# Sixty-four chunk turns ahead of the first FFN: a matmul against a scaled diagonal replaced by a scaling on GpSimd and a transpose on TensorE

## The chip, the cores and the metric

The kernel runs on one core of one Trainium2 chip. The metric is the device time of one execution in microseconds, median of several runs. The kernel before takes 2605.58 us (three runs, 2605.37 to 2605.85).

## The reference

Four sub-layers run one after another over a stream `x` of 1024 tokens by 1024 channels, float32: an HGRN2 mixer, a SwiGLU FFN, a short-convolution mixer, a second FFN. Between the mixer's output and the FFN stands the part that matters here:

```
x  = x + g1 * _rmsnorm(y, norm_w[l, 1])                     # y: output projection of the mixer
hf = _modulate(_rmsnorm(x, norm_w[l, 2]), sh2, sc2)         # h * (1 + scale) + shift, per channel
x  = x + g2 * _rmsnorm(_swiglu(hf, ffn_w_in[l], ffn_w_out[l]), norm_w[l, 3])

def _rmsnorm(x, w):
    xf = x.astype(jnp.float32)
    y = xf * lax.rsqrt(jnp.mean(xf * xf, axis=-1, keepdims=True) + EPS)
    return (y * w.astype(jnp.float32)).astype(x.dtype)
```

The division by a token's root mean square is one number per token; scale and shift are one number per channel. There are 256 context tokens too, in the first mixer alone.

## The kernel before

The stream is held as eight blocks (`LAT` = 8) of 128 tokens by 1024 channels, tokens in the partitions. The FFN wants channels in the partitions, so every block is turned in eight chunks of 128 by 128. Turns are counted by instance: 0 is the input of the first mixer, 1 the first FFN's, 2 the convolution's, 3 the second FFN's. All products are float32 split into a high and a low part, three matmuls for each product (hi times hi, lo times hi, hi times lo). The FFN's products are a Strassen scheme of seven kinds, M1 to M7; each needs its own combination of the input's quarters (`x_terms`), split into high and low.

The norm's factor reaches the block in one of two ways. Where the instance is in `SCALED` (2 and 3), ScalarE writes the block times `x_rstd` into a buffer (`scaled_of`), and TensorE transposes the chunks of that (L1435, `pe.transpose` against `ident`). Instances 0 and 1 leave the block as it is: VectorE writes a diagonal matrix of the 128 factors (L2750, `diag`), and TensorE multiplies every chunk by that (L1436), which scales and turns in one. In the trace such a float32 matmul of one chunk is two records.

Instance 1 runs inside the first output projection. No scheduler decides the order: each engine has its own written list, and semaphores tie them. For block tb of 0 to 7:

- TensorE (`projection_blocks`): wait for `proj_evac` of block tb-2 and for its factor (`diag_done`), `turn_block` of block tb-2 in two halves of four chunks (banks 4 and 5), then what is left of the projection of block tb, `proj_full`. Blocks 6 and 7 are turned at the end: 6 ahead of the first FFN product, 7 inside the third product (`turns_at`).
- ScalarE (`projection`): `y_norm` (square and sum of the projection, square root, `y_std`), `turned_raw` of block tb-1 (eight copies from PSUM with scale and shift into `raw_b`), `x_norm` (the same on the new stream block, `x_std`), then `x_highs` of block tb-1: two for blocks 0 to 3, four for blocks 4 to 7.
- VectorE (`projection`): reciprocal `y_rstd`, `proj_scaled`, the new block `xt`, then `x_sums` of block tb-1 (one, or three from block 4 on), `x_norm` (reciprocal `x_rstd`, and `diag`), `x_lows` of block tb-1 (two, or four).
- GpSimd (`ffn_units`): for the FFN's kind M6, `x6(block)` for blocks 4 to 7, three instructions each (sum, cast to the high part, low part), each as soon as its block's `raw_b` stands. Then the sums and low parts of the weight units.

The FFN's first 14 products run in `FIRST_ORDER`: M2 and M4 of units 0 and 1, then M3, M5, M1, M7, M6. M2 and M4 read blocks 0 to 3 alone; M3, M5, M1, M7 read up to block 7 (`x_ready`), M6 reads what GpSimd made (`x6_ready`). SyncE's queue reloads a slot `xt` for block tb+4 when block tb is turned, and loads the first FFN weights (`ffn_raw`) when all are.

Of the kernel before, what the change touches and what calls it, by code (L numbers as in the profile page):

```python
# [10 lines left out]
ALU = mybir.AluOpType  # L11
# [11 lines left out]
LAT = SEQ // P  # L23
# [64 lines left out]

EARLY_Y, EARLY_SCALE, EARLY_ADD = ({first + 2 * tb: tb for tb in range(4)} for first in (60, 61, 62))
EARLY_X, EARLY_RSTD, EARLY_SCALED = ({first + 2 * tb: tb for tb in range(4)} for first in (63, 64, 65))  # L90
SCALED = 2, 3
CONV_HIGHS = 55, 58
FIRST_TURN = 68

# [92 lines left out]
T0 = (0, 20, 36, 52)  # L187
D0 = (0, 10, 18, 26)
# [3 lines left out]
def turns(inst):  # L192
    return TURNS[(0, 1, 2, 1)[inst]]


def block_turns(inst, block):

    return T0[inst] + 2 * block, T0[inst] + 2 * block + 1
# [92 lines left out]
def normed(inst):  # L291
    return NORMED[0 if inst == 0 else 1]


def blocks_of(q):
    return (8, 9) if q == CTX_Q else (2 * q, 2 * q + 1)


def turned_after(inst, block):

    if inst % 2:
        return block_turns(inst, block)[1] + 1
    return T0[inst] + max(t for t, (q, f) in enumerate(turns(inst)) if block in blocks_of(q)) + 1
# [85 lines left out]
def build_trunk(nc, x, ctx, cond, ada, ada_bias, norm_w, lb_raw, gnorm, conv_w,  # L389
# [8 lines left out]
    def at(name, kib, shape, dt=F32):  # L398
        return nc.alloc_sbuf_tensor_at(name, shape, dt, offset=base + int(kib * 1024))
# [144 lines left out]
    ident = at("ident", 214, [P, P])  # L544
# [4 lines left out]
    def small(name, n):  # L549
        t = at(name, small_at[0], [P, n])  # L550
        small_at[0] += (4 * n + 31) // 32 * 32 / 1024
        return t
# [21 lines left out]
    x_squares, x_std, x_rstd = (small("x_squares", LAT + CCH), small("x_std", LAT + CCH),  # L574
                                small("x_rstd", LAT + CCH))
# [11 lines left out]
    with ctx_mgr:  # L587
# [25 lines left out]
        S = {n: ctx_mgr.enter_context(nc.semaphore(n)) for n in names}  # L613
# [117 lines left out]
        def diag_of(inst, block):  # L731
            i = normed(inst).index(block)
            return diag_start[:, i % 6, :] if inst == 0 else diag[:, i % 4, :]

        def scaled_of(inst, block):

            return ys[0][block // 4][:, block % 4, :] if inst == 2 else x_scaled[block % 3][:, :]

        def stream(inst, block):

            if block >= LAT:
                return ctxt[:, block - LAT, :]
            if inst == 0:
                return x_start[:, block, :]
            return xt_end[0][:, block, :] if inst == 2 else xt_slots[inst // 2][block % 4][:, :]
# [53 lines left out]
        block = ctx_mgr.enter_context(nc.Block())  # L799
# [363 lines left out]
        def _(pool):  # L1163
# [102 lines left out]
            for n in range(4, N_HGRN_OUT):  # L1266
                h, i = n // HEAD_PANELS, n % HEAD_PANELS
# [8 lines left out]
            for half in range(2):  # L1276
# [9 lines left out]
            pool.tensor_tensor(hgrn_rows[KB - 1][1][:, :], last_row_raw[:, :], hgrn_rows[KB - 1][0][:, :], ALU.subtract  # L1286
                               ).then_inc(S["panel_split"], 1)

            def ffn_units(f):

                k0 = PAIR_UNITS * f
# [28 lines left out]

                pool.sem_inc(S["unit_summed"], 2 * len(SUMMED))
                pool.sem_inc(S["unit_ready"], 2 * len(SUMMED))
                if f == 1:
                    pool.wait_ge(S["proj_full"], LAT * (f + 1))
                for block in LATE:
                    x6(block)
# [70 lines left out]
        def _(pe):  # L1397
# [34 lines left out]
            def turn_chunk(out_ap, inst, block, kb):  # L1432

                if inst in SCALED:
                    return pe.transpose(out_ap, chunk(scaled_of(inst, block), kb), ident[:, :])  # L1435
# [634 lines left out]
        def _(act):  # L2070
# [430 lines left out]
            def projection(sub, inst):  # L2501

                f = sub // 2
                if f == 1:
                    out_row_copy(sub)
                act.wait_ge(S["mods_ready"], 2 * inst)
                for tb in range(LAT):
                    act.wait_ge(S["proj_full"], LAT * f + tb + 1)
                    y_norm(sub, tb, proj_of(f, tb), junk_proj[f])
                    if tb > 0:  # L2510
                        turned_raw(inst, tb - 1)
                    act.wait_ge(S["x_updated"], LAT * sub + tb + 1)
                    x_norm(inst, tb, junk_proj[f])
                    if tb > 0:
                        x_highs(f, tb - 1, IN_TIME[f])
                    if inst in SCALED:
                        scale_x(inst, tb)

            def ffn(f):
# [183 lines left out]
        def _(dve):  # L2703
            V = nc.vector
# [28 lines left out]
            def x_norm(inst, block):  # L2733

                n = D0[inst] + normed(inst).index(block)
                c = slice(block, block + 1)
                dve.wait_ge(S["x_std_done"], n + 1)
                V.reciprocal(x_rstd[:, c], x_std[:, c]).then_inc(S["x_rstd_done"], 1)
                if inst in SCALED:
                    return  # L2740
                dve.wait_ge(S["x_rstd_done"], n + 1)
                i = normed(inst).index(block)
                ring_of = 6 if inst == 0 else 4
                if i >= ring_of:
                    dve.wait_ge(S["turned"], turned_after(inst, normed(inst)[i - ring_of]))
                elif inst > 0:
                    dve.wait_ge(S["turned"], T0[inst])
                if inst == 0 and i < 4:
                    return
                V.tensor_scalar(diag_of(inst, block), ident[:, :], x_rstd[:, c], None, ALU.mult  # L2750
                                ).then_inc(S["diag_done"], 1)

            def low(inst, t):
                dve.wait_ge(S["h_hi_done"], H0[inst] + t + 1)
# [61 lines left out]
            for tb in range(4):  # L2816
                x_norm(0, tb)
# [623 lines left out]
```

## Time and profile before

| | |
|---|---|
| device time, median of three | 2605.58 us |
| span of the profiled execution | 2600.0 us |
| TensorE busy (matmuls) | 2524.9 us, 97% |
| VectorE, ScalarE, GpSimd busy | 1750.5, 1122.8, 1245.5 us |
| first output projection and turn of its blocks | about 864 to 935 us of the span |
| FFN products without a pause from | 935.37 us |

The profiled execution's span is 2600.0 us; 5.6 us of the median lie around it. "Busy" of an engine is the time with an instruction in flight; matmuls overlap, so a row's duration (0.39 us) is longer than the step from one to the next (0.23 us). The chain of waits follows the work that ended last back to the start. A timeline lists instructions in order of time, with the idle time ahead of each and what ended it. Line numbers are those of the kernel before; L2707 (VectorE) and L2072 (ScalarE) are helpers, so their rows are told apart by the tile they write.

### The profile page before, as it was taken

The page shows a single profiled execution, that of the slowest core. Times are in us where ns is not written, and L with a number is a line of the kernel's source. Part 1 is how long each engine was busy: PE and PEld are TensorE (multiplying, and loading weights), DVE is VectorE, ACT ScalarE, POOL GpSimd, SP SyncE. Part 2 cuts the span into 40 slices and gives each one's busy share as a digit, 9 for nine tenths or more (in the row PEclk, how much of TensorE's full clock was granted, in tenths as well). Part 3 has the DMA queues.
Part 4 walks back from the last instruction along what each step waited for, and adds up shares of the span by engine and source line. Part 5 has one row for each costly group of instructions (what it writes and reads, how often), then busy time and mean ns, then how long its engine had stood idle before and what let it go on. Part 6 is the DMA issues. An engine that isn't in the chain of part 4 may idle for free.

```text
span 2600.0 us, 35820 instructions
## 1 busy us (share of the span) xinstructions
PE 2524.9 (97%) x12452; PEld 2115.7 (81%) x12452; DVE 1750.5 (67%) x2343; ACT 1122.8 (43%) x2124; POOL 1245.5 (48%) x811
## 2 busy tenths in 40 slices
PE   7999999999999989999999999999999999999998
PEld 5888888888878778888888877888787888888886
DVE  5377777767865566667667986666436555565888
ACT  5334534443443653343445475111264333434444
POOL 3121321432230037776768952444304776766983
PEclk8999999999999999999999999999999999999999
DMA  6223431441361343343456332333514323345533
GB/s 261 74 74 121 178 136 67 154 146 65 114 264 61 138 141 130 122 145 129 165 204 238 97 110 97 115 112 113 214 54 154 106 89 109 116 166 216 191 99 114
DMA packets 119634, 351.05 MB, mean 135 GB/s; under 512 B 12240, under 2 KB 12240, under 8 KB 116432
## 3 DMA queue, kind: packets, MB, share of 16 engines
q1 hardware_dynamic: 119504, 349.33, 38.1%
q8 instruction: 80, 1.31, 0.2%
q14 instruction: 50, 0.41, 0.0%
HBM read 258.58 MB, written 90.70 MB: 134 GB/s over the span
## 4 chain that ended last, share of the span: by engine, by line
PE 83%; DVE 7%; POOL 3%; ACT 3%; DMA 2%; issue 1%; SPq 1%; DVEq 0%; ACTq 0%; POOLq 0%
PE psum L1402 19%; PE psum L1403 19%; PE psum L1404 19%; PE psum L1975 4%; PE psum L1977 4%; PE psum L1976 4%; PE psum L1650 2%; PE psum L1652 2%; PE psum L1651 2%; PE psum L1602 2%; POOL row_unit_sum L1358 2%; PE psum L1616 1%; PE psum L1589 1%; PE psum L1572 1%; DVE k_all L2999 1%
## 5 line engine op out<-in xcount | busy, mean ns | idle before, releaser
L1402 PE MATMUL psum<-x_hi,unit 128*128 128x512 f32 x1232 | 481.5, 391 | 5.2 <-DVE x_lo L2707 5.2
L1403 PE MATMUL psum<-x_lo,unit 128*128 128x512 f32 x1232 | 480.0, 390 | 0.0
L1404 PE MATMUL psum<-x_hi,unit 128*128 128x512 f32 x1232 | 479.9, 390 | 0.0
L2707 DVE TENSOR_TENSOR c_set<-c_set,psum 128x512 f32<-128x512 f32 x352 | 233.8, 685 | 279.3 <-ACT c_set L2072 178.6
L1308 POOL TENSOR_TENSOR unit<-unit_sum,unit 128x512 fp32r<-128x512 f32 x200 | 294.4, 1480 | 5.8 <-ACT unit L2072 4.9
L1402 PEld LDWEIGHTS psum<-x_hi,unit 128*128 128x128 f32 x1232 | 231.9, 188 | 54.2 <-ACT c_set L2072 5.7
L1404 PEld LDWEIGHTS psum<-x_hi,unit 128*128 128x128 f32 x1232 | 231.7, 188 | 48.5
L1403 PEld LDWEIGHTS psum<-x_lo,unit 128*128 128x128 f32 x1232 | 231.9, 188 | 47.6
L1402 PE MATMUL psum<-h_hi,w_hi 128*128 128x512 f32 x624 | 262.6, 421 | 0.2 <-DVE h_lo L2707 0.2
L1975 PE MATMUL psum<-row_unit_hi,part_hi 128*128 128x512 f32 x616 | 241.8, 392 | 3.1 <-DVE part_lo L2707 1.8
L1404 PE MATMUL psum<-h_hi,w_lo 128*128 128x512 f32 x624 | 244.1, 391 | 0.0
L1403 PE MATMUL psum<-h_lo,w_hi 128*128 128x512 f32 x624 | 243.9, 391 | 0.0
L1977 PE MATMUL psum<-row_unit_hi,part_lo 128*128 128x512 f32 x616 | 240.5, 390 | 0.0
L1976 PE MATMUL psum<-row_unit_lo,part_hi 128*128 128x512 f32 x616 | 240.3, 390 | 0.0
L2707 DVE TENSOR_TENSOR part_lo<-part_raw,part_hi 128x512 fp32r<-128x512 f32 x154 | 186.1, 1211 | 64.0 <-ACT part_hi L2072 63.5
L2072 ACT ACTIVATE c_set<-psum 128x512 f32<-128x512 f32 x176 | 100.3, 597 | 265.3 <-PE psum L1404 265.3
L1302 POOL TENSOR_TENSOR unit_sum<-ffn_raw 128x512 f32<-128x512 f32 x80 | 108.6, 1357 | 197.2 <-PE psum L1402 197.2
L1302 POOL TENSOR_TENSOR unit_sum<-ffn_raw,ffn_raw 128x512 f32<-128x512 f32 x120 | 159.8, 1332 | 58.5 <-PE psum L1402 58.0
L1222 POOL TENSOR_TENSOR w_lo<-w_raw,w_hi 128x1024 fp32r<-128x1024 f32 x30 | 73.5, 2449 | 238.6 <-ACT w_hi L2072 238.6
L2072 ACT ACTIVATE unit<-unit_sum 128x512 fp32r<-128x512 f32 x200 | 126.0, 630 | 55.8 <-POOL unit_sum L1302 55.8
L1975 PEld LDWEIGHTS psum<-row_unit_hi,part_hi 128*128 128x128 f32 x616 | 116.1, 188 | 29.4 <-issue 3.4
L1402 PE MATMUL psum<-conv_h_hi,conv_w_hi 128*128 128x512 f32 x352 | 138.1, 392 | 0.4 <-POOL conv_w_lo L1207 0.4
(320 smaller groups left out, 5630.9 us busy)
## 6 DMA issues: line engine op xcount, KB each, us to landing
ffn_raw<-in_w_ffn_in SPq DMA_DIRECT2D x80, 512.0 KB, 5.1
part_raw<-parts_kept SPq DMA_DIRECT2D x154, 256.0 KB, 2.7
parts_kept<-part_sums SPq DMA_DIRECT2D x22, 1280.0 KB, 5.3
out_raw<-in_w_ffn_out SPq DMA_DIRECT2D x44, 512.0 KB, 7.4
w_raw<-in_w_hgrn_in SPq DMA_DIRECT2D x40, 512.0 KB, 3.6
ada_raw<-in_ada SPq DMA_DIRECT2D x32, 512.0 KB, 4.8
conv_ada_raw<-in_ada SPq DMA_DIRECT2D x32, 512.0 KB, 4.1
units_kept<-stage_unit SPq DMA_DIRECT2D x28, 512.0 KB, 2.9
```

The source lines that it names most:

```text
L1222: pool.tensor_tensor(place[1][:, :], w_raws[0][:, slot, :], place[0][:, :], ALU.subtract).then_inc(S["panel_split"], 1)
L1302: pool.tensor_tensor(units[(PRODUCTS * e + l) % 4][2][:, :], one, other, op).then_inc(S["unit_summed"], 1)
L1308: pool.tensor_tensor(unit[1][:, :], unit[2][:, :], unit[0][:, :], ALU.subtract).then_inc(S["unit_ready"], 1)
L1358: pool.tensor_tensor(row_unit(n)[2][:, :], one, other, op).then_inc(S["rows_summed"], 1)
L1402: begin = pe.matmul(out_ap, hi[:, a:b], rhs_hi, start=first, stop=False)
L1403: pe.matmul(out_ap, hi[:, a:b], rhs_lo, start=False, stop=False)
L1404: return begin, pe.matmul(out_ap, lo[:, a:b], rhs_hi, start=False, stop=last)
L1975: begin = pe.matmul(dst, of_hi[:, tokens], hi[:, :], start=g == 0, stop=False)
L1976: pe.matmul(dst, of_hi[:, tokens], lo[:, :], start=False, stop=False)
L1977: return begin, pe.matmul(dst, of_lo[:, tokens], hi[:, :], start=False, stop=g == FFN_GROUPS - 1)
L2072: nc.scalar.activation(dst, src, func, **kw).then_inc(S[sem], 1)
L2707: V.tensor_tensor(dst, a, b, op).then_inc(S[sem], 1)
```

## The change

Instance 1 joins `SCALED`, and GpSimd does the scaling. For each of the eight blocks it waits for `x_rstd`, writes block times factor into one of three buffers `x_scaled` (from the fourth block on also waiting until the block three earlier is turned), and only then TensorE transposes the chunks. VectorE no longer writes `diag` for instance 1. GpSimd does the eight scalings ahead of its twelve `x6` instructions, which so come after the last block's scaling.

```diff
-SCALED = 2, 3
+SCALED = 1, 2, 3
...
+            def scale_x(inst, block):
+                pool.wait_ge(S["x_rstd_done"], D0[inst] + normed(inst).index(block) + 1)
+                if block >= 3:
+                    pool.wait_ge(S["turned"], turned_after(inst, block - 3))
+                pool.tensor_scalar(scaled_of(inst, block), stream(inst, block), x_rstd[:, block:block + 1], None, ALU.mult
+                                   ).then_inc(S["diag_done"], 1)
...
-                if f == 1:
+                if f == 0:
+                    for tb in range(LAT):
+                        scale_x(1, tb)
+                else:
                     pool.wait_ge(S["proj_full"], LAT * (f + 1))
                 for block in LATE:
                     x6(block)
...
-                    if inst in SCALED:
+                    if inst == 3:
                         scale_x(inst, tb)
...
-                if inst in SCALED:
-                    return
-                dve.wait_ge(S["x_rstd_done"], n + 1)
...
+                if inst == 0:
+                    dve.wait_ge(S["x_rstd_done"], n + 1)
...
```

GpSimd's list at the projection, before. `x_6` is the input of kind M6, `raw_b` the turned block with scale and shift:

```order
L1286 TENSOR_TENSOR hgrn_row_96<-last_row_raw,hgrn_row_96 128x1024 [waits w_hi_done]
L1315 TENSOR_TENSOR x_6_sum<-raw_b_137 128x4x128 [waits modulated]
L1317 CAST x_6_hi<-x_6_sum 128x4x128 [waits x6_summed]
L1319 TENSOR_TENSOR x_6_lo<-x_6_sum,x_6_hi 128x4x128 [waits x6_hi]
L1315 TENSOR_TENSOR x_6_sum<-raw_b_137 128x4x128 [waits modulated]
L1317 CAST x_6_hi<-x_6_sum 128x4x128 [waits x6_summed]
```

The same place now:

```order
L1286 TENSOR_TENSOR hgrn_row_96<-last_row_raw,hgrn_row_96 128x1024 [waits w_hi_done]
L1294 TENSOR_SCALAR x_scaled_128<-xt_0_145,x_rstd 128x1024 [waits x_rstd_done]
L1294 TENSOR_SCALAR x_scaled_129<-xt_1_146,x_rstd 128x1024 [waits x_rstd_done]
L1294 TENSOR_SCALAR x_scaled_130<-xt_2_147,x_rstd 128x1024 [waits x_rstd_done]
L1294 TENSOR_SCALAR x_scaled_128<-xt_3_148,x_rstd 128x1024 [waits turned,x_rstd_done]
L1294 TENSOR_SCALAR x_scaled_129<-xt_0_145,x_rstd 128x1024 [waits turned,x_rstd_done]
L1294 TENSOR_SCALAR x_scaled_130<-xt_1_146,x_rstd 128x1024 [waits turned,x_rstd_done]
L1294 TENSOR_SCALAR x_scaled_128<-xt_2_147,x_rstd 128x1024 [waits turned,x_rstd_done]
L1294 TENSOR_SCALAR x_scaled_129<-xt_3_148,x_rstd 128x1024 [waits turned,x_rstd_done]
L1323 TENSOR_TENSOR x_6_sum<-raw_b_137 128x4x128 [waits modulated]
L1325 CAST x_6_hi<-x_6_sum 128x4x128 [waits x6_summed]
```

The eight scalings stand in front, and all twelve `x_6` instructions come behind the eighth.

VectorE's list for one block of the projection, before (`x_0` and `x_1` are the inputs of kinds M2 and M4):

```order
L2707 TENSOR_TENSOR x_1_sum<-raw_b_137 128x4x128 [waits modulated]
L2738 RECIPROCAL x_rstd<-x_std 128x1 [waits x_std_done]
L2750 TENSOR_SCALAR diag<-ident,x_rstd 128x128 [waits turned,x_rstd_done]
L2707 TENSOR_TENSOR x_0_lo<-raw_b_137,x_0_hi 128x4x128 [waits x_hi]
L2707 TENSOR_TENSOR x_1_lo<-x_1_sum,x_1_hi 128x4x128 [waits x_hi]
L2777 RECIPROCAL y_rstd<-y_std 128x1 [waits y_std_done,x_loaded0]
```

and now:

```order
L2718 TENSOR_TENSOR x_1_sum<-raw_b_137 128x4x128 [waits modulated]
L2749 RECIPROCAL x_rstd<-x_std 128x1 [waits x_std_done]
L2718 TENSOR_TENSOR x_0_lo<-raw_b_137,x_0_hi 128x4x128 [waits x_hi]
L2718 TENSOR_TENSOR x_1_lo<-x_1_sum,x_1_hi 128x4x128 [waits x_hi]
L2784 RECIPROCAL y_rstd<-y_std 128x1 [waits y_std_done,x_loaded0]
```

Only `diag` is gone. On TensorE every list position stays, and `L1436 psum<-diag,xt` becomes a transpose `psum<-ident,x_scaled` at the same place with the same waits.

## Rows read from the trace of the kernel before

**Rows 1.** The page: the span.
```profile
span 2600.0 us, 35820 instructions
```
**Rows 2.** Busy time by stretch: bounds, length, each engine, TensorE's granted clock, DMA.
```profile
870.00:920.00 50.00, 39.18 (x192) 30.08 (x191) 41.52 (x60) 45.16 (x108) 8.16 (x6) 0.91 0.42 146
```
**Rows 3.** Chain of waits, one block's round: start, duration, engine, tile.
```profile
885.20 0.30 ACT y_std L2072
885.79 1.30 DVE proj_scaled L2788
...
891.92 0.30 ACT y_std L2072
```
**Rows 4.** VectorE's timeline, block 2's factor: start, duration, instruction, idle before.
```profile
883.16 0.16 DVE L2738 RECIPROCAL x_rstd<-x_std 128x1 f32<-128x1 f32 x1 [0.86 <-ACT x_std L2072]
883.36 0.29 DVE L2750 TENSOR_SCALAR diag<-ident,x_rstd 128x128 f32<-128x128 f32 x1
...
884.29 0.69 DVE L2707 TENSOR_TENSOR x_lo<-x_sum,x_hi 128x512 fp32r<-128x512 f32 x1
885.59 0.17 DVE L2777 RECIPROCAL y_rstd<-y_std 128x1 f32<-128x1 f32 x1 [0.62 <-ACT y_std L2072]
```
**Rows 5.** VectorE's timeline, blocks 4 to 7.
```profile
901.77 3.38 DVE L2707 TENSOR_TENSOR x_sum<-raw_b 128x512 f32<-128x512 f32 x3
...
905.08 0.15 DVE L2738 RECIPROCAL x_rstd<-x_std 128x1 f32<-128x1 f32 x1
905.26 1.10 DVE L2750 TENSOR_SCALAR diag<-ident,x_rstd 128x128 f32<-128x128 f32 x1
...
906.88 1.88 DVE L2707 TENSOR_TENSOR x_lo<-x_sum,x_hi 128x512 fp32r<-128x512 f32 x3
908.69 0.15 DVE L2777 RECIPROCAL y_rstd<-y_std 128x1 f32<-128x1 f32 x1
...
911.33 4.44 DVE L2707 TENSOR_TENSOR x_sum<-raw_b 128x512 f32<-128x512 f32 x3
915.70 0.15 DVE L2738 RECIPROCAL x_rstd<-x_std 128x1 f32<-128x1 f32 x1
...
918.50 0.15 DVE L2777 RECIPROCAL y_rstd<-y_std 128x1 f32<-128x1 f32 x1
...
921.59 3.41 DVE L2707 TENSOR_TENSOR x_sum<-raw_b 128x512 f32<-128x512 f32 x3 [0.36 <-ACT raw_b L2072]
924.92 0.15 DVE L2738 RECIPROCAL x_rstd<-x_std 128x1 f32<-128x1 f32 x1
```
**Rows 6.** GpSimd's timeline at the projection.
```profile
911.24 1.30 POOL L1315 TENSOR_TENSOR x_sum<-raw_b 128x512 f32<-128x512 f32 x1 [4.96 <-ACT raw_b L2072]
...
930.69 1.30 POOL L1315 TENSOR_TENSOR x_sum<-raw_b 128x512 f32<-128x512 f32 x1 [4.54 <-ACT raw_b L2072]
...
955.06 1.29 POOL L1302 TENSOR_TENSOR unit_sum<-ffn_raw 128x512 f32<-128x512 f32 x1 [20.38 <-PE psum L1402]
```
**Rows 7.** TensorE's timeline: turns of blocks 2, 6, 7 (half), and M3's start.
```profile
883.74 2.02 PE L1436 MATMUL psum<-diag,xt 128*128 128x128 f32 x16 [0.18 <-issue]
...
916.23 3.78 PE L1436 MATMUL psum<-diag,xt 128*128 128x128 f32 x16 [4.73 <-DVE diag L2750]
...
926.43 1.06 PE L1436 MATMUL psum<-diag,xt 128*128 128x128 f32 x8
...
935.37 0.47 PE L1402 MATMUL psum<-x_hi,unit 128*128 128x512 f32 x1 [2.19 <-DVE x_lo L2707]
```
**Rows 8.** GpSimd's groups over the whole span: busy us, mean ns of one.
```profile
L1204 POOL TENSOR_TENSOR conv_w_hi<-conv_w_raw,zero 128x1024 fp32r<-128x1024 f32 x22 | 48.4, 2200 | 162.5 <-DMA conv_w_raw<-in_w_conv_in 98.2 <-PE psum L1402 63.7 <-DVE part_lo L2707 0.6
...
L1168 POOL MEMSET cond_pad<- 128x1024 f32 x1 | 1.0, 952 | 0.0
```
**Rows 9.** GpSimd's timeline, a cast that runs alone.
```profile
1950.17 0.61 POOL L1317 CAST x_hi<-x_sum 128x512 fp32r<-128x512 f32 x1
```
**Rows 10.** Chain of waits: four transposes of 128 by 128.
```profile
853.79 0.44 PE psum L1639 x4
```

More of the change, by code:

```diff
@@ L2738, in x_norm @@
                 V.reciprocal(x_rstd[:, c], x_std[:, c]).then_inc(S["x_rstd_done"], 1)
-                if inst in SCALED:
-                    return
-                dve.wait_ge(S["x_rstd_done"], n + 1)
[L2742 to L2751, printed above, removed]
+                if inst == 0:
+                    dve.wait_ge(S["x_rstd_done"], n + 1)
+                    i = normed(inst).index(block)
+                    if i >= 6:
+                        dve.wait_ge(S["turned"], turned_after(inst, normed(inst)[i - 6]))
+                    if i < 4:
+                        return
+                    V.tensor_scalar(diag_of(inst, block), ident[:, :], x_rstd[:, c], None, ALU.mult
+                                    ).then_inc(S["diag_done"], 1)
             def low(inst, t):
```

## The prediction

> **What bounds the kernel now.** I read the page first: TensorE is busy nearly all of the span [rows 1], so a change counts only where TensorE pauses or where work leaves it. Then the busy time by stretch: in 870 to 920 us TensorE is busy for 39.18 of 50 us while ScalarE has 45.16 and VectorE 41.52 [rows 2]; from 935.37 on the FFN's products run without a pause [rows 7]. So the gain or loss of this change is one number: how far the start of M3, at 935.37, moves. Everything behind it is TensorE's own list and moves with it.
>
> Third, the chain of waits inside that stretch. From block 2 on it does not run through TensorE. It is a round between ScalarE and VectorE: `y_std`, then VectorE's `proj_scaled` and `xt`, then ScalarE's `x_norm`, and the next `y_std` 6.72 us later (885.20 to 891.92) [rows 3]. The turns lie beside it: ScalarE picks up block 2's turned chunks just behind `y_std`, at 885.5, and TensorE had begun that turn at 883.74 [rows 7]. From block 4 on the round is longer and VectorE carries it: its three `x_sums` take 3.38, 4.44 and 3.41 us, where three instructions of the same shape take 1.88 when nothing disturbs them [rows 5]. What disturbs them is GpSimd's `x6`, begun at 911.24 beside the sums of 911.33 [rows 6]; a `diag` takes 1.10 us beside it instead of 0.29 [rows 4, 5]. The two engines take turns on whole instructions.
>
> The Trainium skill says the same under SBUF — State Buffer, Who interferes with whom: a VectorE instruction with two SBUF inputs and a GpSimd instruction that reads SBUF block each other for a whole instruction. It speaks against this change too, since the scaling is such an instruction and `x_lows` follow at once; no more comes of it here than the sum below holds already.
>
> **The change, part by part.**
>
> *The transposes.* Four cost 0.44 us [rows 10], so a block 0.88; a block's turn before is sixteen records in 2.02 us at full clock (about 1.8 without the tail that overlaps the next instruction), and 3.78 us for block 6, behind a pause of 4.73 us [rows 7]. TensorE is not what the round waits for, so of some 8 us of TensorE time next to nothing is gained directly; half a turn of block 7 is on the path: 0.44 against 0.9 (half of 1.8), **-0.45**.
>
> *The scaling's price s.* The trace has no such GpSimd instruction. Lower end: a MEMSET of the same width, 0.95 us [rows 8]. A cast of half the width alone takes 0.61 [rows 9]; twice that is 1.22 with its fixed part counted twice. Upper end: a 1024-wide instruction with two operands, one of them a broadcast column, 2.20 us [rows 8]. The scaling has one wide input and one output, as the cast has, so I take **s = 1.1**, and keep 0.95 to 2.2.
>
> The Trainium skill, GPSIMD Engine Reference, Elementwise — side-by-side cycle accounting, gives 1.03 cycles an element for a body of up to two operations and about 1.8 for a tight loop. At 1.2 GHz these are estimates of 0.9 and 1.5 us. The undisturbed cast is nearer the first; by the second the sum would be near zero, which is the second rival.
>
> *Early rounds, the factors of blocks 1 to 4 (four links).* Before, block 2's reciprocal ends at 883.32, the two `x_lows` end at 884.98, and VectorE then idles 0.62 us for `y_std`, starting `y_rstd` at 885.59 [rows 4]. Now GpSimd starts at 883.4 and holds off the `x_lows` until 884.5; these take 0.60 and 0.69 and end at 885.8, so `y_rstd` is late by 0.2. The first half of the turn is there at 884.5 + 0.44 = 884.95, still ahead of ScalarE at 885.5. Four times 0.2: **+0.8**. Block 0's scaling (about 1.1 instead of 0.3) ends within the shorter turn it pays with: 0.
>
> *The three groups of sums.* GpSimd no longer runs `x6` beside them, since all of it stands behind the eighth scaling. (3.38 - 1.88) + (4.44 - 1.88) + (3.41 - 1.88) = **-5.6** [rows 5].
>
> *Late rounds.* From the reciprocal of `x_rstd` to `y_rstd` VectorE now does reciprocal, one `x_low` or the scaling's hold, then the rest: 0.2 + 1.1 + 4 times 0.61 = 3.75. Before it was 905.08 to 908.69 = 3.6 (with a `diag` of 1.10), and 915.70 to 918.50 = 2.8 [rows 5]. **+0.1 and +0.95**. Last, block 7: from the reciprocal at 924.92 to its turn at 926.43 were 1.5 us, of which TensorE's products filled part [rows 5, 7]; now 0.2, up to 0.6 until a running `x_low` lets go, and 1.1: **+0.4**. TensorE comes to this turn earlier too, as block 6's turn is ready about 3 us sooner.
>
> *`x6` behind the scalings.* Four blocks of `x6`, some 4 us each, now run from about 922.5 to 938.5, beside block 6's lows and block 7's add, sum and lows. Before only the last of them did (from 930.69 [rows 6]). The path 926.43 to 935.37 already holds disturbed instructions; more of them can hold it by one or two GpSimd instructions: 0 to 1.5, I take **+0.5**. M6 itself is TensorE's ninth product; with M3 at 932 and four products of 12 times 0.23 us between, it is wanted at 943. GpSimd then has nothing to do until 955 less the gain, where it idled 20.38 us [rows 6]. So the later `x6` costs nothing else.
>
> *The rest.* ScalarE's list is the same. SyncE issues no other DMA; its loads of `xt` slots and of `ffn_raw` wait for turns, which move by less than 1 us for blocks 0 to 3 and come earlier for the last. Removing `diag` from VectorE: 0.29 in the early rounds lay in idle time, the 1.10 is counted in the link.
>
> **Sum:** -0.45 + 0.8 - 5.6 + 0.1 + 0.95 + 0.4 + 0.5 = **-3.3 us**. M3 starts at 932.1, the span is 2596.7; with the 5.6 us that the median has around the profiled span (2605.6 against 2600.0) the time is **2602.3 us**.
>
> With s at 0.95 and nothing for `x6` the sum is about -4.9; s counts in seven links (four early, two late, block 7), so s = 2.2 gives -3.3 + 7 times 1.1 = +4.4.
>
> **The rivals.**
>
> *A, the slower one: GpSimd's scaling becomes the link.* If GpSimd takes the column of factors as a second operand, s is 2.2, or 2.4 with disturbance. For it: the broadcast rows of 2.20 do just that. Against it: the cast. The first half of the turn is then at 883.4 + 2.2 + 0.44 = 886.0, behind ScalarE's 885.5, and the `x_lows` end at 886.9, 1.3 late, each round. The break-even is 1.1 + 3.3/7 = 1.6 us for one scaling; at 2.2 to 2.4 the time is 2610.0 to 2611.5. Chance 0.18.
>
> *B, nothing to be seen:* s of 1.5 to 1.9. -3.3 + 7 times 0.4 to 0.8 = -0.5 to +2.3, 2605 to 2608. Chance 0.20. Here also belongs the case that the gain at M3 is given back later, for which I see no place.
>
> *C, more than forecast:* s near 1.0, `x6` disturbs nothing, and the pauses that put TensorE on the low clock (block 6's 3.78) go away. -4.9 and the 0.36 us wait of VectorE at 921.59 [rows 5], with the shorter pauses: -5 to -6, 2600. Chance 0.14.
>
> *D, `x6` late for M6:* GpSimd would have to end at 943 or later, 4.5 us behind the estimate; each further us comes back. -2 to +1. Chance 0.05.
>
> TensorE, before, came out of each of the pauses ahead of blocks 5 and 6 at a low clock (the stretch's mean grant is 0.91 [rows 2]). The Trainium skill, TensorE: Matmul & The Clock Gate, PE-mode transpose, says that transposes do not count as busy to the clock gate, which would leave the first products at 1.2 GHz a little longer. The products ahead of block 7's turn have to wait for its scaling in any case, so it would change neither sum nor chance.
>
> **How the numbers follow.** The forecast (s up to 1.4, -4.9 to -1.2) has 0.43. A measurement of this kernel can tell about 0.2%, 5.2 us, from no change. Faster by more: most of C, and a little of the forecast whose terms all err to one side, 0.15. Slower by more needs s over 2.3, or A with more disturbance: 0.15. Within: 0.70. The range 2599.9 to 2610.0 leaves out the better half of C and the worse half of A.
>
> **What would show it.** Right: GpSimd rows `x_scaled` near 1.1 us; the three `x_sums` near 1.9 us each group; reciprocals `x_rstd` of blocks 5, 6, 7 at about 904.5, 913, 921.5 instead of 905.08, 915.70, 924.92; M3 near 932. Wrong: scaling rows of 1.6 us and more with rounds longer than 7 us in blocks 1 to 4; sums still over 3 us; TensorE waiting for `x_6_lo` at M6; or M3 early and the second half of the kernel longer.

## The result: eleven microseconds slower

The changed kernel takes 2616.51 us (median of 4 runs, 2614.58 to 2616.71) against 2605.47 us of the kernel before on the same chip (4 runs, 2604.93 to 2605.85): ratio 1.0044, 95% interval 1.0032 to 1.0056. The forecast was 2602.3 us, its range ended at 2610.0. Both the number and the sign were wrong.

The page of the changed kernel, its span, to set beside [rows 1]:

```profile
span 2615.0 us, 35689 instructions
```

Busy time by stretch, changed kernel (bounds, length, TensorE, its weight loads, VectorE, ScalarE, GpSimd, granted clock, DMA), beside [rows 2]:

```profile
870.00:920.00 50.00, 33.72 (x136) 22.88 (x135) 33.52 (x44) 37.87 (x92) 17.98 (x6) 0.93 0.46 158
```

Every engine but GpSimd has less to show for the same 50 us: ScalarE 37.87 instead of 45.16, VectorE 33.52 instead of 41.52. Fewer rounds fit into the stretch. What fills the time stands in GpSimd's timeline (start, duration, instruction, idle time before and what ended it):

```profile
881.24 2.85 POOL L1294 TENSOR_SCALAR x_scaled<-xt,x_rstd 128x1024 f32<-128x1024 f32 x1 [5.33 <-DVE x_rstd L2749]
889.41 2.85 POOL L1294 TENSOR_SCALAR x_scaled<-xt,x_rstd 128x1024 f32<-128x1024 f32 x1 [5.33 <-DVE x_rstd L2749]
...
914.38 3.75 POOL L1294 TENSOR_SCALAR x_scaled<-xt,x_rstd 128x1024 f32<-128x1024 f32 x1 [5.77 <-DVE x_rstd L2749]
```

One scaling takes **2.85 us**, where the forecast had 1.1 and at most 2.2. The first five take that, the last three 3.75, with a group of three of VectorE's lows beside them. The scalings follow each other at 8.17 us (881.24 to 889.41), where a round was 6.72 before [rows 3]. The chain of waits of the stretch names who carries it:

```profile
877.84 1.75 ACT raw_b L2083 x5
879.58 1.05 ACT junk_proj L2083 x2
...
880.65 0.30 ACT x_std L2083
...
880.98 0.17 DVE x_rstd L2749
...
881.24 2.85 POOL x_scaled L1294
```

Before, the chain went from ScalarE's `y_std` to VectorE's `proj_scaled` and back, with the turns beside it [rows 3]. Its round of 6.72 us is as long as ScalarE's own list of one block; in ScalarE's timeline of the kernel before no row of that round has idle time ahead of it:

```profile
885.40 2.89 ACT L2072 ACTIVATE raw_b<-psum,mods,in_scale 128x128 f32<-128x128 f32 x8
888.37 1.06 ACT L2072 ACTIVATE junk_proj<-xt 128x1024 f32<-128x1024 f32 x1
...
892.13 2.89 ACT L2072 ACTIVATE raw_b<-psum,mods,in_scale 128x128 f32<-128x128 f32 x8
```

Now the chain goes reciprocal, scaling, turn, `raw_b`, `x_norm`, and the next block's reciprocal. ScalarE's timeline shows the turn as what it waits for, and TensorE's shows the turn right behind the scaling:

```profile
883.02 0.29 ACT L2083 ACTIVATE y_std<-y_squares,eps 128x1 f32<-128x1 f32 x1
884.85 2.91 ACT L2083 ACTIVATE raw_b<-psum,mods,in_scale 128x128 f32<-128x128 f32 x8 [1.54 <-PE psum L1446]
...
888.83 0.29 ACT L2083 ACTIVATE x_std<-x_squares,eps 128x1 f32<-128x1 f32 x1
```

```profile
884.19 1.06 PE L1446 MATMUL psum<-ident,x_scaled 128*128 128x128 f32 x8 [2.60 <-issue]
...
937.65 0.66 PE L1446 MATMUL psum<-ident,x_scaled 128*128 128x128 f32 x4
...
946.87 0.77 PE L1413 MATMUL psum<-x_hi,unit 128*128 128x512 f32 x1 [3.32 <-DVE x_lo L2718]
```

**The ring.** Scaling from 881.24 to 884.09, first half of the turn, `raw_b` from 884.85, `x_norm` behind it, `x_std` at 888.83, reciprocal at 889.15, next scaling at 889.41. All of it but the scaling is 8.17 - 2.85 = 5.32 us. So the ring is s + 5.32 (s is the price of one scaling, as in the prediction), and it replaces the round of 6.72 as soon as s is above 1.4. The forecast gave each early round only what `x_lows` and `y_rstd` lose to a running GpSimd instruction.

What was meant to be gained did come. VectorE's timeline, against the 4.44 and 3.41 of [rows 5]:

```profile
912.32 1.90 DVE L2718 TENSOR_TENSOR x_sum<-raw_b 128x512 f32<-128x512 f32 x3 [1.64 <-ACT raw_b L2083]
914.13 0.16 DVE L2749 RECIPROCAL x_rstd<-x_std 128x1 f32<-128x1 f32 x1
914.81 2.73 DVE L2718 TENSOR_TENSOR x_lo<-x_sum,x_hi 128x512 fp32r<-128x512 f32 x3
...
933.60 0.15 DVE L2749 RECIPROCAL x_rstd<-x_std 128x1 f32<-128x1 f32 x1
```

**A better mark than M3.** The forecast measured everything by the start of M3, since "everything behind it is TensorE's own list and moves with it". GpSimd's first `unit_sum` waits for a product behind M3. It started at 955.06 before [rows 6], 19.69 us behind M3, and now at 968.41, 21.54 us behind:

```profile
968.41 1.29 POOL L1310 TENSOR_TENSOR unit_sum<-ffn_raw 128x512 f32<-128x512 f32 x1 [15.11 <-PE psum L1413]
```

The stretches behind M3 of the changed kernel say why: TensorE was busy all the time, but the clock granted to it was low at first (a mean of 0.63 of full speed over 4.5 us).

```profile
946.87:951.37 4.50, 4.50 (x13) 3.62 (x14) 4.50 (x5) 1.26 (x2) 4.35 (x4) 0.63 0.38 117
951.37:955.87 4.50, 4.50 (x22) 3.72 (x21) 2.67 (x4) 2.51 (x3) 1.85 (x2) 1.00 0.72 243
```

and the same 4.5 us of the kernel before:

```profile
935.37:939.87 4.50, 4.50 (x20) 3.75 (x21) 3.55 (x6) 2.71 (x4) 0.00 (x0) 1.00 0.46 140
```

Thirteen matmuls instead of twenty, seven of 0.23 us: some 1.6 us are lost behind M3's start. So below the stage is measured from the first `y_rstd` of the projection (865.89 before, 868.51 now) to the first `unit_sum`: 89.17 us before, 99.90 after, **+10.7**, close to the 11.0 between the times. Measured from its own trace's `y_rstd`, the stage leaves out what varies ahead of it: that reciprocal starts anywhere between 865.7 and 869.0 us in the fourteen traces of this study, although the kernels don't differ ahead of it. What lies behind `unit_sum` varies too, by 2.4 us (1644.7 to 1647.1).

### The profile page after: what moved, and what is told of

Read it like the earlier page. It is cut to its first block, busy times and chain, and to the rows that moved or that the text cites. A ratio compares the mean times of both kernels' runs of the same rounds, so it can differ in the third digit from the quotient of the medians.

```text
span 2615.0 us, 35689 instructions
## 1 busy us (share of the span) xinstructions
PE 2527.5 (97%) x12388; PEld 2113.1 (81%) x12388; DVE 1750.0 (67%) x2335; ACT 1121.8 (43%) x2124; POOL 1269.5 (49%) x819
## 4 chain that ended last, share of the span: by engine, by line
PE 82%; DVE 6%; POOL 4%; issue 3%; ACT 3%; DMA 2%; SPq 1%; DVEq 0%; ACTq 0%; POOLq 0%
PE psum L1413 19%; PE psum L1415 19%; PE psum L1414 19%; PE psum L1986 4%; PE psum L1988 4%; PE psum L1987 4%; PE psum L1661 2%; PE psum L1663 2%; PE psum L1662 2%; PE psum L1613 2%; POOL row_unit_sum L1369 2%; PE psum L1600 1%; PE psum L1627 1%; PE psum L1583 1%; DVE k_all L3006 1%
## 5 line engine op out<-in xcount | busy, mean ns | idle before, releaser
L1222 POOL TENSOR_TENSOR w_lo<-w_raw,w_hi 128x1024 fp32r<-128x1024 f32 x30 | 73.1, 2437 | 238.4 <-ACT w_hi L2083 238.4
```

The source lines that it names most:

```text
L1222: pool.tensor_tensor(place[1][:, :], w_raws[0][:, slot, :], place[0][:, :], ALU.subtract).then_inc(S["panel_split"], 1)
```

## The experiments

Theory 1: the loss comes from the price of the scaling instruction, through the ring. Rivals: moving `x6` costs it, or GpSimd standing in the ring costs it at any price, or the transposes do. All differences of time are against the kernel before on the same chip. The stage is cut into four parts, each as change against before, in us: **early** from `y_rstd` to block 4's reciprocal `x_rstd` (30.72 before), **late** from there to block 7's (28.31), **last** from there to M3 (10.45), **clock** from M3 to `unit_sum` (19.69).

| kernel | one scaling | round | early | late | last | clock | stage | time |
|---|---|---|---|---|---|---|---|---|
| changed | 2.85 GpSimd | 8.17 | +6.27 | -0.21 | +2.82 | +1.85 | +10.73 | +11.0 |
| changed_again | 2.85 | 8.17 | +6.64 | -0.17 | +2.83 | +1.84 | +11.14 | +11.3 |
| x6_between | 2.84 | 8.16 | +6.41 | +0.50 | +1.96 | +1.95 | +10.82 | +9.6 |
| two_operand | 1.89 | 7.48 | +3.22 | -2.93 | +1.18 | +1.91 | +3.38 | +2.4 |
| half_scales | 1.57 | 6.90 | +1.16 | -3.61 | +1.92 | +1.94 | +1.41 | +1.2 |
| copy_scales | 1.04 | 6.72 | +0.07 | -5.35 | +0.31 | +1.90 | -3.07 | -2.4 |
| act_scales | 1.13 ScalarE | 7.76 | +3.91 | -2.69 | +1.31 | +1.42 | +3.95 | +5.9 |
| dve_scales | 0.75 VectorE | 6.72 | -0.24 | -5.78 | +1.61 | +1.65 | -2.76 | -2.3 |
| no_scaling | none | 6.72 | -0.58 | -5.82 | +0.75 | +2.45 | -3.20 | -3.4 |
| x6_late | diag as before | 6.72 | -0.01 | -5.81 | +2.65 | +3.06 | -0.11 | -2.5 |
| late_fill | diag as before | 6.72 | 0.00 | -5.81 | +2.55 | +0.10 | -3.16 | -2.4 |
| dve_fill | 0.75 VectorE | 6.72 | -0.24 | -5.76 | +1.52 | +0.05 | -4.43 | -3.4 |

The stage comes from one trace, the time from medians whose runs lie 4 to 7 us apart; they agree within about 2.5 us throughout. Differences of time up to some 3.5 us reach the edge of their intervals or lie within them, so comparisons as fine as that rest on the stage. The kernel with ten more GpSimd instructions (prices, below) was run once and serves for its rows alone. The rows below are those on which a verdict rests.

**The price by itself.** The kernel before, with ten GpSimd instructions of five forms behind block 0's reciprocal.

```diff
+forms = (lambda: pool.tensor_scalar(dst[:, :], src[:, :], col, None, ALU.mult),
+         lambda: pool.tensor_scalar(dst[:, :], src[:, :], 2.0, None, ALU.mult),
+         lambda: pool.tensor_scalar(dst[:, 0:HALF], src[:, 0:HALF], col, None, ALU.mult),
+         lambda: pool.tensor_copy(dst[:, :], src[:, :]),
+         lambda: pool.tensor_tensor(dst[:, :], src[:, :], col.broadcast_to([P, D]), ALU.mult))
```

> The kernel before with ten GpSimd instructions put into its idle time ahead of the first x6, each waiting for the one before, on a buffer of ones: twice tensor_scalar 1024 wide with a column of factors, the same with a constant, 512 wide with the column, tensor_copy 1024, tensor_tensor against the broadcast column. If the price of 2.85 us is the column's, the constant is near the copy (about 1.1); if it is tensor_scalar's own, the constant takes 2.85 too; 512 columns give 1.5 either way; the tensor_tensor 1.9.

GpSimd's timeline, the first of two rows for each form:

```profile
873.34 2.85 POOL L1331 TENSOR_SCALAR x_scaled<-x_scaled,x_rstd 128x1024 f32<-128x1024 f32 x1
876.27 2.77 POOL L1332 TENSOR_SCALAR x_scaled<-x_scaled 128x1024 f32<-128x1024 f32 x1
879.14 1.60 POOL L1333 TENSOR_SCALAR x_scaled<-x_scaled,x_rstd 128x512 f32<-128x512 f32 x1
880.80 1.10 POOL L1334 COPY x_scaled<-x_scaled 128x1024 f32<-128x1024 f32 x1
881.99 1.90 POOL L1335 TENSOR_TENSOR x_scaled<-x_scaled,x_rstd 128x1024 f32<-128x1024 f32 x1
```

The price belongs to the operation: 2.77 with a constant, 2.85 with the column. A copy, which moves the same bytes, takes 1.10, and the form with two operands 1.90. The second row of each form, in the same order, is 4.22, 2.77, 1.98, 1.04 and 2.35 us: VectorE was at work beside all ten instructions, and beside the longest of them, from 883.98 on, it ran a sum, a `diag` and two lows. 2.85 is thus the lower of two values, and the one that the first five scalings of the changed kernel show. The forecast had taken the cast as the nearest row, with "one wide input and one output, as the cast has". For GpSimd the count of inputs does not order these forms. The Trainium skill, GPSIMD Engine Reference, Elementwise — side-by-side cycle accounting, gives 1.03 cycles an element for a body of up to two operations and 2.6 for two inputs; at 1.2 GHz these are estimates of 0.9 and 2.2 us. The copy is near the first. The scaling, one operation on one wide input, stands at three times it, and there the measurement decides against the page. The two-operand form stands below the second, but its second operand is a broadcast column. With two full inputs of this width the kernel before has `w_lo<-w_raw,w_hi` (GpSimd, L1222, 30 rows), 2.38 us and more, which agrees with the second.

**The scaling in other forms, at its place.**

```diff
-pool.tensor_scalar(scaled_of(inst, block), stream(inst, block), x_rstd[:, block:block + 1], None, ALU.mult
-                   ).then_inc(S["diag_done"], 1)
+pool.tensor_tensor(scaled_of(inst, block), stream(inst, block),              # two_operand
+                   x_rstd[:, block:block + 1].broadcast_to([P, D]), ALU.mult).then_inc(S["diag_done"], 1)
+pool.tensor_copy(scaled_of(inst, block), stream(inst, block)).then_inc(S["diag_done"], 1)   # copy_scales
```

> The changed kernel with the scaling written as a tensor_tensor against the broadcast column of factors, which took 2.2 us in other places of this kernel, instead of 2.85. Theory 1 (the scaling's duration s counts in some seven links): 7 times 0.65 = 4.5 us under the changed kernel, about 2612. Theory 2 (not the scaling): no difference, 2616.5.

> The changed kernel with GpSimd's eight scalings replaced by plain copies of the block into the same buffers, at the same places and with the same waits. It leaves out the norm's factor on the first FFN's input. A copy of this size took 1.10 us undisturbed in the run of single prices, which is the price the prediction assumed for a scaling. Theory 1 (only the price of the instruction makes the change slow): the ring is 1.10 + 5.32 = 6.42 us, under the round of 6.72 us, so blocks 1 to 4 keep 6.72 us, the groups of three sums stay at 1.9 us, the reciprocals of blocks 5, 6 and 7 end near 904.5, 912.5 and 921, M3 starts near 931 to 932.5, and the time is 3 +- 1.5 us below the kernel before, as forecast for s = 1.1. Theory 2 (that GpSimd stands in the ring at all costs, whatever its price, by taking turns with VectorE): rounds over 7 us, M3 behind 935, time at or above the kernel before.

> The changed kernel with GpSimd scaling only the first four chunks of a block (512 columns, 1.60 us undisturbed in the run of single prices); the last four chunks are transposed from the block itself, so half of the channels lack the norm's factor. The ring is 1.60 + 5.32 = 6.92 us, just above 6.72. Theory 1: rounds of blocks 1 to 4 of 6.9 to 7.2 us, so 1 to 2 us are lost there and the gain of the sums just about pays for it: M3 at 933 to 936, time within 2 us of the kernel before, between copy_scales and two_operand (1.90 us, rounds 7.48, M3 939.6). Theory 2 (no threshold, each microsecond counts from zero): four rounds longer than those of copy_scales by the whole 0.5 us each.

Times: two_operand 2606.5 us against 2604.06, ratio 1.0013 (1.0004 to 1.0022); half_scales 2605.85 against 2604.68, 1.0006 (0.9997 to 1.0015); copy_scales 2602.33 against 2604.68, 0.9991 (0.9982 to 1.0). GpSimd's timeline in half_scales:

```profile
884.45 1.56 POOL L1294 TENSOR_SCALAR x_scaled<-xt,x_rstd 128x512 f32<-128x512 f32 x1 [5.32 <-DVE x_rstd L2749]
891.35 1.57 POOL L1294 TENSOR_SCALAR x_scaled<-xt,x_rstd 128x512 f32<-128x512 f32 x1 [5.33 <-DVE x_rstd L2749]
```

and in copy_scales, with VectorE's last lows there:

```profile
886.54 1.04 POOL L1294 COPY x_scaled<-xt 128x1024 f32<-128x1024 f32 x1 [5.68 <-DVE x_rstd L2748]
893.26 1.04 POOL L1294 COPY x_scaled<-xt 128x1024 f32<-128x1024 f32 x1 [5.68 <-DVE x_rstd L2748]
```

```profile
920.91 1.89 DVE L2717 TENSOR_TENSOR x_sum<-raw_b 128x512 f32<-128x512 f32 x3
922.72 0.15 DVE L2748 RECIPROCAL x_rstd<-x_std 128x1 f32<-128x1 f32 x1
924.44 4.49 DVE L2717 TENSOR_TENSOR x_lo<-x_sum,x_hi 128x512 fp32r<-128x512 f32 x3
```

Rounds of 6.90 at 1.57 (1.57 + 5.33) and of 6.72 at 1.04 (where s + 5.32 would be 6.36) agree with a threshold at 1.4. No price between 1.04 and 1.57 was run. At 1.04 GpSimd idles 5.68 instead of 5.33 us: the older round is back in charge. So theory 1 holds and "GpSimd in the ring at any price" falls. The sizes expected held for copy_scales and half_scales; for two_operand about 2612 us was expected by seven links of 0.65, and it took 2606.5, about twice that gain; its scalings were cheaper by 0.96 us early and by 1.86 in the last three blocks (1.89 for 3.75), not by 0.65. two_operand's rounds of 7.48 are 0.27 above 1.89 + 5.32. VectorE's and ScalarE's timelines show the forecast's other mechanism there:

```profile
888.16 2.16 DVE L2718 TENSOR_TENSOR x_lo<-raw_b,x_hi 128x512 fp32r<-128x512 f32 x1 [0.36 <-ACT x_hi L2083]
...
893.62 1.06 ACT L2083 ACTIVATE junk_proj<-xt 128x1024 f32<-128x1024 f32 x1 [0.17 <-DVE xt L2718]
```

Beside GpSimd's instruction (887.89 to 889.78) an `x_lo` of 0.69 takes 2.16 us, `y_rstd` and `xt` follow it late, and `x_norm`, which read a waiting `xt` in the ring, now waits for it. With copies nearly the forecast's own case was run (1.04 for s = 1.1). Of its four early links, 0.2 each, the last lies behind block 4's reciprocal and so in the late part. Early is +0.07 where +0.6 was forecast, late -5.35 where -4.35 was, last +0.31 where +0.45 was, and then +1.90 behind M3, where nothing was.

**The same kernel once more.**

> The changed kernel once more, unaltered, beside the two others on one chip: 9 to 12 us slower than the kernel before, scalings of 2.85 us, rounds of 8.17 us in blocks 1 to 4, M3 near 946.9. It shows how far the start of M3 and the time move from one profile to another, as a measure for the differences read between the variants.

2615.98 us against 2604.68, ratio 1.0040 (1.0025 to 1.0056). Its stage differs by 0.4 us from the first trace, in one early round of 8.54 us, whose turn took 1.85 us instead of 1.06. That is the measure for the table's differences.

**`x6` alone, and `x6` back in between.**

```diff
                 if f == 1:
                     pool.wait_ge(S["proj_full"], LAT * (f + 1))
+                else:                                              # x6_late, in the kernel before
+                    pool.wait_ge(S["x_rstd_done"], D0[1] + LAT)
...
                     for tb in range(LAT):
                         scale_x(1, tb)
+                        if tb > 4:                                 # x6_between, in the changed kernel
+                            x6(tb - 1)
+                    x6(LAT - 1)
```

> The kernel before with one edit: GpSimd waits for the eighth x_rstd before its first x6 instruction. Diagonals and matmuls stay. Theory 1 (the changed kernel lost by the price of GpSimd's scaling; putting x6 back was a gain as forecast): the three groups of x_sums fall from 3.38, 4.44, 3.41 us to about 1.9 each, M3 starts 5 to 6 us sooner, time 5 to 6.5 us under before. Theory 2 (x6 behind the last block is what cost): M3 or M6 waits, time 3 us or more over before.

> The changed kernel with x6 of block 4 behind the scaling of block 5, of block 5 behind that of block 6, of block 6 behind that of block 7, instead of all behind the eighth. Theory 1 (the price of the scaling, 2.85 us in a ring scaling, turn, raw_b, x_norm, x_rstd): nothing of that ring changes, time within 3 us of the changed kernel's 11 over before. Theory 2 (x6 standing behind the last scaling holds up VectorE ahead of M3): 4 us or more better than the changed kernel.

x6_late: 2601.52 us against 2604.06, ratio 0.9991 (0.9982 to 1.0). x6_between: 2613.66 against 2604.03, 1.0038 (1.0024 to 1.0052). VectorE's timeline of x6_late:

```profile
917.32 1.90 DVE L2709 TENSOR_TENSOR x_sum<-raw_b 128x512 f32<-128x512 f32 x3
...
919.32 1.43 DVE L2752 TENSOR_SCALAR diag<-ident,x_rstd 128x128 f32<-128x128 f32 x1
...
921.27 4.47 DVE L2709 TENSOR_TENSOR x_lo<-x_sum,x_hi 128x512 fp32r<-128x512 f32 x3
```

Moving `x6` alone gives the -5.8 us of the late part, and x6_between, with the price of 2.85 and `x6` early, is as slow as the changed kernel. So the move isn't the loss. (x6_between has -0.86 of the changed kernel's last part and +0.71 in the late one.) But the move fell short of the 5 to 6.5 us expected of it, and took 2.5: it takes part of its gain back twice: the last block's `diag` takes 1.43 and its lows 4.47 us beside `x6` (last +2.65, where the forecast had +0.5 for `x6`), and the rest goes to the clock, below.

**The scaling on other engines, or none.** act_scales lets ScalarE write `x_scaled` as it does for instance 3; dve_scales puts this on VectorE in place of `diag`:

```diff
+V.tensor_scalar(scaled_of(inst, block), stream(inst, block), x_rstd[:, c], None, ALU.mult
+                ).then_inc(S["diag_done"], 1)
```

no_scaling transposes the block itself; its first FFN's input lacks the norm's factor.

> ScalarE writes the scaled block for instance 1 (as it does for instances 2 and 3, 1.14 us each) and GpSimd does x6 after the eighth x_rstd; TensorE transposes. Theory 1: the scaling is cheap as latency but ScalarE is the engine that is full in the rounds of blocks 1 to 4, so these grow by up to 1.1 us each; with the freed sums the time ends 0 to 4 us over before. Theory 3 (only the latency of the scaling counts, not whose list it stands in): 1.1 us is what was forecast for GpSimd, so 2 to 4 us under before.

> VectorE writes the scaled block in place of the diagonal (0.5 us for 512 columns elsewhere, so 0.7 to 0.8 here, against 0.29), x6 after the eighth x_rstd, TensorE transposes. Theory 1: the ring stays under ScalarE's round of 6.72 us; VectorE had 0.6 us to spare in each early round; so like the kernel with only x6 moved, 1 to 3.5 us under before. If transposes in place of diagonals cost by themselves, over before.

> The changed kernel without the scaling: TensorE transposes the unscaled blocks as soon as x_rstd is there, x6 after the eighth x_rstd; the norm's factor is left out of the first FFN's input. It has the shorter turns and the late x6, and no price at all. Theory 1: 5 to 7 us under before, about 2599. Theory 2: still 5 us or more over before.

act_scales: 2609.92 us against 2604.03, ratio 1.0020 (1.0010 to 1.0029). dve_scales: 2601.71 against 2604.03, 0.9986 (0.9977 to 0.9996). no_scaling: 2600.7 against 2604.06, 0.9987 (0.9978 to 0.9997). ScalarE has no idle time in act_scales' early rounds, one of which is 7.76 us:

```profile
888.43 1.14 ACT L2082 ACTIVATE x_scaled<-xt,x_rstd 128x1024 f32<-128x1024 f32 x1
...
896.20 1.13 ACT L2082 ACTIVATE x_scaled<-xt,x_rstd 128x1024 f32<-128x1024 f32 x1
```

That is 6.72 plus the 1.04 from one ScalarE row to the next, so in this kernel ScalarE's list sets the early round. act_scales was expected to end 0 to 4 us over the kernel before and ended 5.9 over; dve_scales came as expected. The transposes cost nothing that these rows show; with the whole change done by VectorE at 0.75 us a block, the early rounds stay at 6.72. And even with no scaling at all, only 3.2 us are to be had in this stage, where 5 to 7 were expected: M3 starts 5.65 us sooner, and 2.45 of it are lost behind.

**The clock behind the last pause.** late_fill is x6_late, and dve_fill dve_scales, with twelve matmuls in TensorE's list ahead of the wait for M3's input. They write the bank that M3's first product overwrites.

```diff
                         if first and kb == 0:
+                            if f == 0 and kind == M3:
+                                for _ in range(12):
+                                    pe.matmul(bank(b), units[slot][0][:, 0:P], xs[f][M2][0][:, 0, :], start=True, stop=True)
                             x_done(kind)
```

> x6_late (the kernel before with only GpSimd's x6 behind the eighth factor) with twelve matmuls of 128x512 more in TensorE's list right ahead of its wait for M3's input, into the bank that M3 overwrites; they use weights and an input that are there. In x6_late M3 started 3.2 us sooner than before (counted from the first y_rstd of its own trace), behind a pause of 2.76 us, and then TensorE ran about 6 us at a granted clock of 0.50, so that GpSimd's first unit_sum, which waits for a product behind M3, came at the same distance as before (89.06 against 89.17 us). Theory 1 (the gain at M3 was given back by the clock that fell after the pause): twelve matmuls at full clock last 2.7 us and fill the pause; M3 starts where it did (66.3 us after y_rstd), at a granted clock of 1.00, unit_sum comes 2.5 to 3 us sooner (86.3), and the time falls by another 2 to 3 us, 4 to 5 below the kernel before. Theory 2 (the late x6 or VectorE's copies hold M3's first products, or the clock falls whatever TensorE does): granted clock of M3 and the distance to unit_sum as in x6_late, same time or a little more.

> The same twelve matmuls in dve_scales (the change's transposes, VectorE doing the scaling, x6 behind the last factor), where M3 started 65.07 us after y_rstd behind a pause of 3.10 us and unit_sum came at 86.41, M3's first 16 us having a mean grant of 0.89. Theory 1: grant 1.00, unit_sum at about 84.7, time 1.5 to 2 us below dve_scales, that is 4 to 4.5 below the kernel before, and the fastest kernel of this study together with late_fill. Theory 2: no difference to dve_scales.

late_fill: 2601.88 us against 2604.3, ratio 0.9989 (0.998 to 0.9998). dve_fill: 2600.89 against 2604.3, 0.9989 (0.998 to 0.9998). TensorE in x6_late, M3's start, and the 12 us behind it by stretches:

```profile
932.23 0.76 PE L1404 MATMUL psum<-x_hi,unit 128*128 128x512 f32 x1 [2.76 <-DVE x_lo L2709]
```

```profile
932.23:938.23 6.00, 6.00 (x14) 4.74 (x15) 4.84 (x5) 1.77 (x3) 3.54 (x3) 0.50 0.28 90
938.23:944.23 6.00, 6.00 (x27) 4.89 (x27) 2.57 (x4) 2.00 (x3) 0.00 (x0) 0.99 0.86 313
```

The same in late_fill:

```profile
929.72 2.88 PE L1946 MATMUL psum<-x_hi,unit 128*128 128x512 f32 x12
...
932.67 0.50 PE L1404 MATMUL psum<-x_hi,unit 128*128 128x512 f32 x1
```

```profile
932.67:938.67 6.00, 6.00 (x26) 4.95 (x27) 5.57 (x6) 3.03 (x4) 3.68 (x3) 1.00 0.53 184
```

With the pause filled the granted clock stays at 1.00 (2.4 GHz), 26 matmuls pass instead of 14 at 0.50 (1.2 GHz), and `unit_sum` comes 19.79 us behind M3 instead of 22.75, although `x6` and VectorE work beside it as before. In dve_fill it is 19.74 instead of 21.34. The cause of the loss behind M3 is thus shown for these two kernels: the low clock behind the pause. In the changed kernel the pause was not filled; its +1.85 is put down to the same cause by its grant of 0.63 there, and not tested. In all ten traces with a pause of 2.35 to 4.33 us ahead of M3 the grant is low behind it and the clock part is +1.4 to +3.1. The Trainium skill, TensorE: Matmul & The Clock Gate, What's actually happening, says that the slow clock is the default and activity releases it; the rows agree. The kernel before has a pause of 2.19 us at this place too [rows 7], and prices one of 2.21, and neither shows a fall of the clock behind it. What sets the two apart, the length of this pause or the idle time before, was not tested.

In the time the fill doesn't show. For dve_fill 4 to 4.5 us under the kernel before were expected: the medians give -3.4 against -2.3 of dve_scales, but the ratios 0.9989 against 0.9986, the other way round, and each interval holds both. For late_fill the expected further 2 to 3 us didn't show: 2.4 us under the kernel before, as x6_late (2.5). x6_late's one trace has its `unit_sum` no sooner than before, but its median is 2.5 us lower; that its other runs lost less to the clock than the profiled one would explain this, and wasn't tested.

## Why the prediction was wrong

- **The scaling's price s** is the step that failed. Forecast 1.1, bounds 0.95 and 2.2; measured 2.85, and 3.75 for the last three. Put into the prediction's own rule that s counts in seven links, 2.85 gives 2602.3 + 7 times 1.75 = 2614.6 us, 1.9 below the measured time. So in total the sum was nearly as sensitive to s as the kernel is (13.8 us of stage between 1.04 and 2.85, 7.6 for each microsecond); what it had wrong beside the price is how the loss comes about, and where. The upper bound was a row of another operation [rows 8] taken as worse than the unseen one, as it has an operand more. Its 2.20 is a mean of rows of 1.89 to 2.88, and undisturbed that form takes 1.89, so even the bound was no bound for the slower form. Rival A, which had "GpSimd's scaling becomes the link" at 2.2 to 2.4, had the mechanism, at a chance of 0.18, and ended at 2611.5 (by its own sum 2611.4) for the same reason.
- **Early rounds.** Forecast +0.8 in four links, of which three, +0.6, lie in the part measured here; measured +6.3. The forecast followed the scaling into VectorE's `x_lows`, and compared the turn with ScalarE's `y_std` once. It didn't close the ring back to the next reciprocal. Closed, with s = 2.85, it gives 8.17 - 6.72 = 1.45 a round, 5.8 in four. The rest comes from the first round, which was shorter before, and is 8.17 now like the others.
- **Sums freed: right.** 1.90 us each instead of 3.38, 4.44 and 3.41. Forecast -5.6; x6_late, where nothing else changes, has -5.81 in the late part.
- **Late links.** +0.1 and +0.95 forecast. The late part as a whole came to -0.21; less the -5.6 of the sums, +5.4. It holds one scaling of 2.85 and two of 3.75, none of 1.1.
- **Block 7, the transposes and `x6`.** -0.45 + 0.4 + 0.5 = +0.45 forecast, +2.82 measured. From the reciprocal at 933.60 to the turn at 937.65 are 4.05 us instead of 1.51. For the price of 1.04 it is +0.31 (copy_scales). Where VectorE does the last block's `diag` or scaling beside `x6`, the last part is at or over the 1.5 us allowed for `x6`: +1.5 to +2.65.
- **"Take turns on whole instructions"**, which sized the early links at 0.2, is not what the scaling does (last section); a two-operand instruction does.
- **"Everything behind it moves with it"** was wrong by 1.85 us. That sentence made M3's start the measure, and so a pause's clock fell out of the sum. The clock was written down for the turn of block 6, not for M3.
- **Time around the span.** The forecast added 5.6 us, the median less the profiled span. The changed kernel's profiled run took 2616.67 for a span of 2615.0, so 1.7 lie around it; by the same 1.7 the profiled run of the kernel before took about 2601.7 (an estimate; its own time is not on record), below its four timed runs. The rest of the 5.6 is then that it was profiled in one of its shorter runs.
- **Rival D** (`x6` late for M6) didn't occur: M6 isn't preceded by a pause of TensorE in any of the traces with `x6` late.

Had s been 1.1, the forecast would have stood: copy_scales, with 1.04, took 2602.33 us, 2.4 under the kernel before on its chip. But that agreement is partly luck. It has two errors in it that cancel, a stage that gave 1.7 us more up to M3 (-4.97 for -3.3) and 1.9 us lost behind.

## What to carry to other kernels

Before a step is put on another engine, close the ring that it will stand in: from its end over every consumer back to its own next start, and set that sum beside the round of now; the difference of the two is the price at which the loss begins (here 1.4 us; in the stage the move gained 3.1 us at 1.04 and lost 1.4 at 1.57). An operation that no row of the trace shows has no upper bound from a row of another operation, least of all on GpSimd; measure it alone first. And a gain at the end of a pause counts only where TensorE comes out of it at full clock: take the mark behind the next matmuls, not at the first.

## What the runs showed of the hardware

- GpSimd, 128x1024 float32, lower of two rows each: `tensor_scalar` 2.85 us with a column, 2.77 with a constant, 1.60 for 512 columns; `tensor_tensor` with the column broadcast 1.90; copy 1.04. The same product by a two-operand instruction is a third cheaper, and in this kernel was worth 7.4 us of the stage.
- The forecast said that VectorE and GpSimd "take turns on whole instructions". Beside `tensor_scalar` they don't. In the changed kernel the scaling of 881.24 to 884.09 keeps its 2.85 us and has both lows inside it; the first is held for some 0.7 us, the second not at all (VectorE's timeline):

```profile
881.50 1.40 DVE L2718 TENSOR_TENSOR x_lo<-raw_b,x_hi 128x512 fp32r<-128x512 f32 x1 [0.36 <-ACT x_hi L2083]
882.82 0.68 DVE L2718 TENSOR_TENSOR x_lo<-x_sum,x_hi 128x512 fp32r<-128x512 f32 x1
```

  In two_operand the first low ends 0.54 us after the GpSimd instruction of 1.89 (2.16 us, above), as if it had waited for most of it. The Trainium skill, SBUF — State Buffer, Who interferes with whom, lets one block the other for a whole instruction; the two-operand form agrees, the scaling doesn't. In prices a scaling of 4.22 us has a sum, a `diag` and two lows beside it, all four at their undisturbed 0.68, 0.29 and 0.69 us: there it is the scaling that gets longer. So its price acted through the turn, and hardly by holding VectorE off.
- Beside a group of three lows the scaling takes 3.75 us instead of 2.85, and the lows 2.73 instead of 1.88.
- M3's first 6 us ran at a grant of 0.50 behind a pause of 2.76 us and at 1.00 behind twelve matmuls whose result nobody reads: 3.0 us of the stage for a filled pause, though the medians of the time don't show them.
- dve_fill has the shortest stage of these kernels that compute the whole reference, 15.2 us under the changed kernel (10.73 + 4.43). Its time is 3.4 us, 0.1%, under the kernel before, which the runs can't tell from late_fill, dve_scales or x6_late.
